# MoE dispatch in a two-layer decoder trunk: token rows scattered by place into one expert-sorted buffer and transposed by VectorE, in place of a table of token ids

## What is computed

```
aff = sigmoid(x @ router_w)                 # 512 x 16 experts
# best of 4 groups, then the best two experts of it: expert[n, 0..1]
gate = aff[expert] / sum(aff[expert])
for each expert e, for the rows x_e that chose it:
    y = (silu(x_e @ w_gate[e]) * (x_e @ w_up[e])) @ w_down[e]     # 1024 -> 512 -> 1024
out[n] = gate[n,0] * y[n, expert 0] + gate[n,1] * y[n, expert 1]
x = layer_norm(alpha * x + out)
```

## Time and profile before

| | |
|---|---|
| median of 3 runs | 1277.02 us (1270.77 to 1279.67) |
| the profiled execution, its own time | 1279.67 us |
| its span, first to last instruction | 1279.7 us |
| TensorE busy | 1033.9 us (81%) |
| VectorE busy | 485.0 us (38%) |
| ScalarE busy | 168.2 us (13%) |
| GpSimd busy | 199.6 us (16%) |
| DMA read and written in HBM | 252.48 MB and 21.80 MB |
| convolution of the last chunks on TensorE ends | 203.3 us |
| experts of layer 0, first to last product | 328.0 to 621.6 us |
| experts of layer 1 | 938.1 to 1233.4 us |

### The profile page before, as it was taken

How to read it: one execution, slowest core, us unless ns; L and a number is a source line. 1 busy time by engine, 2 the same in 40 slices (tenths; PEclk the granted TensorE clock), 3 DMA queues, 4 the chain that set the end, 5 groups by cost and what they waited for, 6 DMA issues and landing times.

```text
span 1279.7 us, 15066 instructions
## 1 busy us (share of the span) xinstructions
PE 1033.9 (81%) x5458; PEld 552.4 (43%) x5459; DVE 485.0 (38%) x1003; ACT 168.2 (13%) x375; POOL 199.6 (16%) x257
## 2 busy tenths in 40 slices
PE   5999597993799889999488899968369777999950
PEld 3444244542455445455134444534245444555520
DVE  1799991446111011101285456564510000110117
ACT  0000002212000000000103332432200000000010
POOL 2243601112200100100241002021210010000013
PEclk8999798986799999999788799878679898999985
DMA  9930011206399999988790001300738999897863
GB/s 296 401 116 0 0 66 66 82 34 223 116 345 380 356 401 338 381 290 361 253 323 39 1 1 66 148 1 34 246 104 314 382 391 390 296 378 294 359 217 112
DMA packets 59726, 275.04 MB, mean 215 GB/s; under 512 B 5469, under 2 KB 13833, under 8 KB 51352
## 3 DMA queue, kind: packets, MB, share of 16 engines
q1 hardware_dynamic: 40368, 226.50, 47.1%
q10 hardware_dynamic: 12952, 28.03, 5.9%
q0 software_dynamic: 6352, 19.77, 5.1%
HBM read 252.48 MB, written 21.80 MB: 214 GB/s over the span
## 4 chain that ended last, share of the span: by engine, by line
PE 60%; DMA 14%; DVE 12%; issue 9%; POOL 2%; ACT 2%; SPq 0%; DVEq 0%; ACTq 0%; POOLq 0%
PE ps L616 20%; PE ps L626 10%; PE ps L755 5%; DMA wring<-in_moe_w_gate_dram 5%; DMA wring<-in_moe_w_up_dram 5%; PE ps L552 5%; PE ps L526 4%; PE ps L774 4%; PE ps L609 3%; DVE arena L898 2%; DMA wring<-in_conv_w_dram 1%; PE ps L514 1%; POOL vareps L1590 1%; DVE bns L917 1%; PE ps L800 1%
## 5 line engine op out<-in xcount | busy, mean ns | idle before, releaser
L616 PE MATMUL ps<-wring,arena 128*64 128x256 f32 x2624 | 314.3, 396 | 40.1 <-DMA wring<-in_moe_w_gate_dram 18.3
L616 PEld LDWEIGHTS ps<-wring,arena 128*64 128x64 f32 x2624 | 195.2, 143 | 154.3 <-issue 54.6
L626 PE MATMUL ps<-wring,arena 128*64 128x512 f32 x688 | 157.0, 598 | 6.8 <-DVE arena L1108 5.7
L898 DVE SCALAR_TENSOR_TENSOR arena<-arena,dwT 128x512 f32<-128x512 f32 (+1 forms) x174 | 125.4, 799 | 0.0
L514 PE MATMUL ps<-arena,wring 128*128 128x512 f32 x256 | 113.1, 604 | 9.3 <-DMA wring<-in_conv_w_dram 9.3
L1095 DVE COPY arena<-ps 128x256 f32<-128x256 f32 x32 | 13.6, 425 | 239.6 <-PE ps L670 239.6
L755 PE MATMUL ps<-wring,arena 128*128 128x512 f32 x192 | 91.0, 631 | 6.3 <-DMA wring<-in_attn_wq_dram 2.9
L626 PEld LDWEIGHTS ps<-wring,arena 128*64 128x64 f32 x688 | 46.1, 136 | 85.3 <-issue 74.9
L514 PEld LDWEIGHTS ps<-arena,wring 128*128 128x128 f32 x256 | 49.4, 194 | 71.6 <-issue 71.6
L526 PE MATMUL ps<-arena,wring 128*128 128x512 f32 x124 | 55.9, 614 | 12.9 <-DVE arena L883 12.9
L1590 POOL TENSOR_SCALAR vareps<-mv 128x1 f32<-128x1 f32 x20 | 21.6, 1082 | 274.0 <-DVE mv L919 273.9
(11 more groups left out here) (209 smaller groups left out, 933.0 us busy)
## 6 DMA issues: line engine op xcount, KB each, us to landing
wring<-in_moe_w_up_dram SPq DMA_DIRECT2D x32, 2048.0 KB, 20.7
wring<-in_moe_w_down_dram SPq DMA_DIRECT2D x32, 2048.0 KB, 13.4
wring<-in_moe_w_gate_dram SPq DMA_DIRECT2D x30, 2048.0 KB
y_dram<-arena ACTq DMA_DIRECT2D x86, 128.0 KB, 8.1
wring<-in_conv_w_dram SPq DMA_DIRECT2D x8, 1024.0 KB, 11.7
wring<-in_conv_w_dram SPq DMA_DIRECT2D x2, 2048.0 KB, 17.8
y_dram<-arena ACTq DMA_DIRECT2D x1, 4096.0 KB, 27.7
x_dram<-x_sb ACTq DMA_DIRECT2D x8, 512.0 KB, 3.1
```

Of the source, the lines that this page charges most:

```text
L616: mm = pe.matmul(ps[h * CAP:(h + 1) * CAP, bank, 0:256], act[:, k, :], w[:, k, h * 256:(h + 1) * 256], start=(k == 0), stop=(k == KD - 1))
L626: mm = pe.matmul(ps[h * CAP:(h + 1) * CAP, bank, :], act[:, j % 2, (j // 2) * CAP:(j // 2 + 1) * CAP], w[:, j, h * 512:(h + 1) * 512], sta ...
L898: dve.scalar_tensor_tensor(out=acc, in0=hpad[:, one, k:k + S], scalar=dwT[:, one, k:k + 1], in1=acc, op0=ALU.mult, op1=ALU.add).then_inc(s ...
```

## The change

The table of token ids, the copy of x in x_dram and y_dram go. One buffer in HBM, xs_dram, has 512 rows for each of the 16 experts, 8,192 rows of 4 KB.

- `later_loads` fills all of xs_dram with zeros, from a new tile `zero`, by one DMA of 8,192 rows (L1298 before, L1227 now) where it filled 1,024 rows of y_dram. ScalarE no longer waits for the fill; GpSimd's first scatter does (s_xinit).
- The scatter writes each token's row of x, 4 KB, to its place, instead of its 4-byte number. Reading back and turning the table goes, with the stores to x_dram.
- A tile of 64 tokens is read as a plain piece of xs_dram by four DMAs of 32 partitions (`fetch`), so that VectorE can turn it by one instruction of 32x32 blocks from SBUF to SBUF (`turned`). TensorE's transposes of tiles go. VectorE's `copy_t` for expert e+1 now stands ahead of `gated` for e.
- Products are stored over the rows of x that they came from, and place_i serves for gathering them too; the arithmetic for rowi goes.
- ScalarE's scaling of x_sb waits for the scatters instead of the stores.

The core of the diff:

```diff
+    xs_dram = nc.dram_tensor("xs_dram", [E * S, D], F32).ap()
+    xs_tiles = xs_dram.rearrange("(n h c) (q d) -> q c n h d", h=2, c=QROWS, q=QUADS)
...
@@ scalar, later_loads
-                act.dma_start(y_dram[E * CAP:, :].rearrange("(p n) (h d) -> p (n h) d", p=P, h=2),
-                              cv[:, KD - 1, :].unsqueeze(1).to_broadcast([P, (TBLK - E) * CAP // P * 2, S])
-                              ).then_inc(s_yinit, 16)
+                act.dma_start(xs_dram.rearrange("(p n) (h d) -> p (n h) d", p=P, h=2),
+                              zero[:, :].unsqueeze(1).to_broadcast([P, E * S // P * 2, 512])).then_inc(s_xinit, 16)
...
-            act.wait_ge(s_yinit, 16)
...
@@ tensor, step of an expert
                     stage_u(e, eh, b, True)
-                    if not last:
-                        stage_t(e + 1, eh + b, 1 - b)
                     stage_y(e - 1, eh if b else eh - 1, 1 - b, later=not first_h)
...
@@ tensor, extras
-                            pe.wait_ge(s_oxg, gathered)
-                            pe.wait_ge(s_xgT, copied)
-                            gathered_T(xg[2], s_oxt)
-                            pe.wait_ge(s_oxgT, now)
+                            pe.wait_ge(s_oxgT, now + 1)
...
@@ vector, experts
+                def turned(i):
+
+                    return dve.transpose(xgT[i].rearrange("p k (h c) -> p h k c", h=2),
+                                         xg[i].rearrange("p h (c k) -> p h k c", k=KD))
+
+                def copy_t(e, eh, b, later):
+                    arrived = in_register(dve, r_dve, 16 * QUADS * (eh + (W0 + 1)))
+                    dve.wait_ge(s_xg[b], arrived)
                     if later or l > 0:
                         dve.wait_ge(s_up, e + (M0 - 1))
-                    dve.tensor_copy(xgT[b].rearrange("p a b -> p (a b)"), ps[:, 0, :]).then_inc(s_xgT, 1)
+                    turned(b).then_inc(s_xgT, 1)
...
                     copy_h(e - 1, 1 - b, True)
+                    if not last:
+                        copy_t(e + 1, eh + b, 1 - b, True)
                     gated(e, b, True)
-                    if not last:
-                        copy_t(e + 1, 1 - b, True)
                     extras(e)
...
@@ gpsimd
                 if l == 0 and t == 0:
-                    pool.wait_ge(s_tokinit, 16)
+                    pool.wait_ge(s_xinit, 16)
                 pool.wait_ge(s_place, T * l + t + 1)
                 for j in range(2):
-                    pool.indirect_dma_start(out=tok_dram[:, :],
+                    pool.indirect_dma_start(out=xs_dram[:, :],
                                             out_offset=bass.IndirectOffsetOnAxis(ap=place_i[:, j, t:t + 1], axis=0),
-                                            in_=tokid[:, t:t + 1], in_offset=None).then_inc(s_scat, 16)
-
-            def token_table(l):
-                pool.wait_ge(s_scat, 16 * 2 * T * (l + 1))
-                pool.dma_start(tok_r[:, :], tok_dram.rearrange("(p n) a -> p (n a)", p=E * NBLK)).then_inc(s_tokr, 16)
-                pool.wait_ge(s_tokT, l + 1)
...
+                                            in_=x_sb[:, t, :], in_offset=None).then_inc(s_scat, 16)
+
+            def fetch(where, n, signal):
+                for q in range(QUADS):
+                    pool.dma_start(where[q * QROWS:(q + 1) * QROWS, :, :], xs_tiles[q, :, bass.ds(n, 1), :, :]
+                                   ).then_inc(signal, 16)
...
                 def gather(e, b, later):
                     if later or l > 0:
-                        pool.wait_ge(s_xt, e + (M0 - 1))
-                    pool.tensor_copy(idx[:, b:b + 1], tokT[:, bass.ds(e * NBLK, 1)]).then_inc(s_idx, 1)
-                    count = in_register(pool, r_pool, e + (M0 + 1))
-                    pool.wait_ge(s_xst, 16 * T * (l + 1))
-                    pool.wait_ge(s_idx, count)
-                    gather_x(xg[b], b, s_xg[b])
+                        pool.wait_ge(s_xgT, e + (M0 - 1))
+                    fetch(xg[b], e * NBLK, s_xg[b])
```

More of the change, by code:

```diff
@@ L194, in trunk @@
         oT = [view(11264 + i * D, KD, P) for i in range(2)]
-        xg = [view(i * D, D) for i in range(3)]
+        xg = [view(i * S, 2, D // QUADS) for i in range(3)]
         xgT = [view(3072 + i * S, KD, CAP) for i in range(3)]
@@ L476, in _ @@
             g = ctx.enter_context(pe.register("pe_extra"))
-            r_pe = [ctx.enter_context(pe.register(f"pe_r{i}")) for i in range(2)]
             pe.reg_mov(g, 1)
@@ L601, in _ @@
             stage_r(T - 1)
-            def token_table(l):
-                pe.wait_ge(s_tokf, l + 1)
-                pe.transpose(ps[0:CAP, 1, 0:E * NBLK], tok_f[:, :], ident[:, :]).then_inc(s_tokt, 1)
-            def gathered_T(src, signal):
-                for j in range(KD):
-                    last = pe.transpose(ps[:, 0, j * CAP:(j + 1) * CAP], src[0:CAP, j::KD], ident[0:CAP, 0:CAP])
-                last.then_inc(signal, 1)
             def half_products(bank, act, w, signal, first=None):
@@ L999, in places @@
                     dve.wait_ge(s_rank, t + 1)
-                own(dve.tensor_tensor(r1[:, :], ps[:, bank, 0:E], tbase[:, :], ALU.add))
+                if t == T - 1:
+                    dve.tensor_copy(cntf[:, 0, :], ps[:, bank, E:2 * E])
+                taken_from = s_rankc if l == 0 else bank_read[bank - 5]
+                dve.tensor_tensor(r1[:, :], ps[:, bank, 0:E], tbase[:, :], ALU.add).then_inc(taken_from, 1)
+                if l == 0:
+                    dve.wait_ge(s_rankc, t + 1)
+                else:
+                    taken(dve, ("R", t))
                 own(dve.tensor_tensor(r2[:, :, :], onehot[:, :, t, :], r1[:, :].unsqueeze(1).to_broadcast([P, 2, E]),
@@ L1004, in places @@
                 dve.tensor_copy(place_i[:, :, t], placef[:, :]).then_inc(s_place, 1)
-                if t == T - 1:
-                    dve.tensor_copy(cntf[:, 0, :], ps[:, bank, E:2 * E])
-                kept = dve.tensor_copy(rankf[:, t, :], ps[:, bank, 0:E])
-                kept.then_inc(s_rankc if l == 0 else bank_read[bank - 5], 1)
-                if l == 0:
-                    dve.wait_ge(s_rankc, t + 1)
-                else:
-                    taken(dve, ("R", t))
             def table(l):
-                count, more, first, shift = (cntf[:, i, :] for i in range(4))
+                count, more = (cntf[:, i, :] for i in range(2))
                 shape = [P, E, NBLK - 1]
@@ L1371, in store @@
                     for h in range(2):
[L1372 removed]
+                        act.dma_start(xs_dram[bass.ds(e * S, CAP), h * 512:(h + 1) * 512],
                                       ysb[b][h * CAP:(h + 1) * CAP, :]).then_inc(s_y[b], 16)
@@ L1387, in extras @@
                             for h in range(2):
-                                act.dma_start(y_dram[bass.ds(row, CAP), h * 512:(h + 1) * 512],
+                                act.dma_start(xs_dram[bass.ds(row, CAP), h * 512:(h + 1) * 512],
                                               ysb[2][h * CAP:(h + 1) * CAP, :]).then_inc(s_oy, 16)
@@ L1533, in _ @@
                                pattern=[[1, P]], channel_multiplier=-1)
-            own(pool.memset(before[:, :, :], 1.0))
-            pool.affine_select(out=before[:, :, :], in_=before[:, :, :], compare_op=ALU.is_gt, fill=0.0, base=0,
-                               pattern=[[1, E], [-1, E]], channel_multiplier=0)
             own(pool.memset(mask[:, :], 0.0))
```

153 lines of the change are left out of this document (35 added, 118 removed).

## The result

The changed kernel takes **1232.26 us** (median of 4 runs, 1231.42 to 1233.29), the kernel before 1275.80 us in the runs beside it (4 runs, 1270.77 to 1279.67). The ratio is **0.9648, 95% interval 0.9618 to 0.9679**: faster by 3.5%. The forecast was 1313 us with a range of 1240 to 1335, so the time lies outside it and on the other side of no change.

What follows compares the result with a forecast made beforehand. It took TensorE (60% of the chain) and DMA (14%) as bounds, by stretch, with VectorE pacing the early convolution. Fill +68.5, expert stages -28, dispatch -4 gave +36.5 on 1279.7, less 2.7 for the median: 1313 us, range 1240 to 1335.

Steps and rivals of the forecast that it cites:

- ScalarE is free when only what fits is left ... I take 136: Start: issuing the xs_dram fill holds ScalarE until 136 us (bounds 132 to 149), delaying VectorE's second gated unit: +68.5 us.
- what is beyond that is issued as fast as it drains: Fill on ScalarE's queue: about 4.2 MB, perhaps half as much again, fits; issuing the remainder proceeds at the drain rate.
- The forecast of 216 for the matmuls: Convolution: TensorE's run of 124 matmuls (L526) would start near 216 us in place of 147.
- The rule of the Trainium skill: Fill's issue: many descriptors can be emitted before incremental cost shows, so the fill would cost nothing; the prediction sided against it.
- the first rival: Start: the fill is taken at once, without holding ScalarE, giving 1277 - 28 - 4 = 1245 us; chance 0.17.
- The landing of the fill: Start: the 33.6 MB zero fill of xs_dram, at 400 GB/s beside a 2.1 MB load, lands at 149 us.
- The expert stages, -28: Both expert stages: TensorE loses 51 us of transposes and copy waits, weight loads limit the gain to 28 (bounds -10, -51).
- the forecast's mark: Late stretches of the expert stages: DMA's share would be 0.95 or more, from 0.90 and 0.86.
- The block transpose: Expert tiles: VectorE's block transpose replaces its copy, taken as 0.70 us and covered by TensorE's products.
- The fetch in four issues: Expert tiles: four GpSimd issues in place of one, on a queue with about 20 us between tiles, cost nothing.
- The dispatch, -2 in each layer: Scatter to first expert product: rows scattered directly, products from about 325 instead of 328.00 us; -4 in all (bounds -6, +6).
- Regular steps of 11.0 instead of 12.0 us: Expert stages: steps of an expert without a further tile would take 11.0 us instead of 12.0.

## Why the prediction was wrong, step by step

- **"ScalarE is free when only what fits is left ... I take 136": the step that failed.** The sum charged +68.5 us for it, and the measured charge is nothing: the second sigmoid came at 51.51 us. The hold exists, but the prediction had it on the wrong issue. It read the earlier trace rows as "what is beyond that is issued as fast as it drains", a price in bytes that the transfer itself pays. What is held is the next issue on the queue. With one issue behind the fill, ScalarE was held until 141.2 us (forecast 136, bounds 132 to 149), the matmuls started at 217.39 and the time was 1304.7.
- **What the trace of the kernel before could have told.** The eight loads of L400 are eight issues, and the earlier trace rows gave only their sum. One by one the 26.75 us are 0.74, 1.48, 8.55, 3.95, 2.78, 3.13, 3.05 and 2.77: the first two went through almost at once, and each of the others stood until 4.5 to 7 us before the load ahead of it landed. The issue of 5.68 us in the earlier trace rows stood behind three others as well. Read so, the 0.66 us of the earlier trace rows needed no depth of the queue to explain it: that fill was the last in its queue, and so is the 32 MB one. The question to ask was what stands behind L1298 on ScalarE's queue. The time line after the change answers it: the next DMA there is issued at 302.73 us, long after the fill has landed.
- **The forecast of 216 for the matmuls, met at 217.39 with a load behind the fill, is in part luck.** The hold ended 5.2 us later than 136, with the second gated unit at 142.33 instead of 137.1. From there to the matmuls it took 75.06 us, where 78.8 were forecast. In that run one chunk of taps took 21.9 us instead of 25.3, because no GpSimd instruction lay beside its last add: the add took 0.69 us instead of 4.09. The prediction had given back 3.2 us for GpSimd in one chunk; 3.4 more fell away in another.
- **The rule of the Trainium skill** ("DMA: Bandwidth & Descriptors", in its part on the anatomy of one DMA, there for GpSimd's path), that many descriptors can be emitted before their cost shows, agrees with the issue of the fill, 0.66 us for 16,384 pieces of 2 KB. It says nothing of the issue behind it, which stood 97.28 us. The prediction gave the first rival 0.17; its time, 1245 us, is 13 us above the result.
- **The landing of the fill**: 148.5 us, forecast 149. The working by bytes and rate held.
- **The expert stages, -28**: right in mechanism, too small; measured 39.6. The cut on TensorE was taken as 51 and is about 59, since a step loses 1.18 us and not 1.03, and a further tile 2.0 and not 1.8. The weights take 20 of it, forecast 23. So the term that was mis-sized here is the cut itself, by 8 of the 11.6 us. DMA's share did go to 0.97 and 0.92 in the late stretches, from 0.90 and 0.86; the forecast's mark was 0.95 or more, so it held in one.
- **The block transpose**: 1.10 us, taken as 0.70. Its cover held at that price too: no step waits for it (its two waits are each layer's first). The fetch in four issues cost 4 x 0.535 us of a queue that nothing waited for, as forecast.
- **The dispatch, -2 in each layer**: -4.1 in the first, of which 1.5 lies ahead of the last scatter, and about -2.5 in the second. The scatter took 6.50 us instead of 5.29 and the transpose 1.10 instead of 0.70. Against that, the last quarter was issued 2.0 us behind the scatter's landing instead of 3.0, it landed in 2.20 us instead of 2.5, and the microsecond for GpSimd's own queue was not needed. In the second layer the last scatter took 7.95 us.
- **Regular steps of 11.0 instead of 12.0 us**: as forecast, where no load is waited for.
- **What stays open.** The end of the program: the last normalisation ends 41.0 us after the last product in both kernels and the output's store is issued right behind it and lands in 2.6 and 2.7 us, yet the span ends 2.9 us later after the change (46.2 to 46.4 us from the last product in the four profiles with the code of before, 47.9 to 49.5 in the ten with that of after). No row shows by what.

With nothing behind the fill to be held, the prediction's own terms would have read 1277 - 28 - 4 = 1245; with the measured 39.6 of the stages and 6.6 of the two dispatches (4.1 and 2.5) they give 1231.

## What to carry to other kernels

Before pricing a large transfer on the queue of an engine that also computes, ask what is issued behind it on the same queue. Here 32 MB were cheap to issue, and the next issue paid, even with 2 KB. So let such a transfer go last, and do not cut it into pieces that follow each other. A sum over several issues ("x8") hides which of them waited; look at each. And when work is taken off an engine beside transfers that are nearly full, price the whole step's difference first and then what the transfers take of it: here 59 us became 40.

## What the runs showed of the hardware

- An issue on ScalarE's queue took 0.46 to 0.66 us whether it stood for 4, 16 or 32 MB. The next one, of 2 KB, waited until about 6 us before the 32 MB landed (141.2 and 146.9 us); with halves of 16 MB the second was released 8.5 us ahead of the first one's landing, with pieces of 4 MB each 7.7 to 9.5 us ahead.
- SP's eight loads of 1 MB at the start took 26.13 us to issue after the change (26.75 before): the same hold is in both kernels. The second of them took only 1.48 us (before) and was let through 9.2 us ahead of the first one's landing. Whether bytes, pieces or something else decides when the next issue is let through is open.
- VectorE's block transpose of 128x512 with a strided source took 1.08 to 1.12 us in each of 43 cases, against 0.69 for the plain copy from PSUM that it replaced.
- VectorE's add of 128x512 at the end of a chunk of taps took 0.69 us with no GpSimd instruction beside it. With one it took 2.81 us (L846 at 64.33 us, changed kernel) and 4.09 us (L901 at 115.58 and 140.92 us, kernel before), and ended 0.5 us after that instruction each time.
- A fill of 32 MB beside the convolution, with 389 and 401 GB/s moved in the two stretches above, changed neither VectorE's nor TensorE's time there: the run of 124 matmuls starts at 147.34 us, before 147.37.
